# Reordering the four-tile borders of a two-block transformer kernel: which engine scales which operand block, and when

## The reference

```python
def adaln_in(s, g_pre, shift, scale):
    return rmsnorm(s, g_pre) * (1 + scale) + shift
def adaln_out(s, y, g_post, gate, weight):
    return s + weight * gate * rmsnorm(y, g_post)
def ffn_sublayer(s, mod, j, g_pre, g_post, wg, wu, wd):
    y = adaln_in(s, g_pre, mod[..., 3 * j, :, :], mod[..., 3 * j + 1, :, :])
    return adaln_out(s, swiglu(y, wg, wu, wd), g_post, mod[..., 3 * j + 2, :, :], FFN_RES)
for l in range(DEPTH):          # for x and, but for the last sublayers, for the context h
    x = ffn_sublayer(x, mod_x, 0, *f0)
    ...                         # a mixer: gMLP, differential attention, window attention
    x = ffn_sublayer(x, mod_x, 2, *f1)
```

## Time and profile before

| | |
|---|---|
| Median of 3 runs (lowest, highest) | 2495.48 us (2495.12, 2497.25) |
| The profiled execution: time, span | 2497.8 us, 2496.0 us |
| TensorE matmul busy | 2414.0 us (97%) |
| VectorE busy | 1143.2 us (46%) |
| ScalarE busy | 1021.4 us (41%) |
| GpSimd busy | 166.4 us (7%) |
| Mean share of the DMA queue of the weights (16 engines) | 41.6% |
| Mean granted clock of TensorE, of full speed | 0.989 |

### The profile page before, as it was taken

The page is one execution under the profiler, slowest core; times in us unless marked ns, Lnnn a source line. Parts: engine busy times, 40 slices in busy tenths (PEclk is TensorE's granted clock), DMA queues, the critical chain, the costliest instruction groups (busy, mean ns, idle before and its releaser), DMA issues. The chain is left out here.

```text
span 2496.0 us, 29214 instructions
## 1 busy us (share of the span) xinstructions
PE 2414.0 (97%) x11296; PEld 1898.3 (76%) x11296; DVE 1143.2 (46%) x1900; ACT 1021.4 (41%) x1766; POOL 166.4 (7%) x205
## 2 busy tenths in 40 slices
PE   8999999999999999999989999999999999988998
PEld 6876788766877778877677777887778887766777
DVE  5654465634552223363656222345322335456555
ACT  6544456534542222354545222234322234445444
POOL 1200003000010000013001000001000000310000
PEclk9999999999999999999989999999999999999999
DMA  6567654387535442232104444332532222322554
GB/s 213 189 231 277 234 186 152 121 309 279 187 129 185 172 140 93 85 97 98 51 18 143 178 169 169 102 101 85 175 123 99 93 85 93 119 68 77 184 187 143
DMA packets 118728, 364.34 MB, mean 146 GB/s; under 512 B 11072, under 2 KB 11712, under 8 KB 118592
## 3 DMA queue, kind: packets, MB, share of 16 engines
q1 hardware_dynamic: 116336, 355.62, 41.6%
q0 software_dynamic: 2256, 6.86, 1.0%
HBM read 361.35 MB, written 1.09 MB: 145 GB/s over the span
## 5 line engine op out<-in xcount | busy, mean ns | idle before, releaser
L1680 DVE TENSOR_TENSOR wlo<-raw,whi 128x1024 fp32r<-128x1024 f32 x524 | 644.0, 1234 | 731.6 <-ACT whi L1119 727.4
L1119 ACT CAST whi<-raw 128x1024 fp32r<-128x1024 f32 x524 | 548.2, 1050 | 621.2 <-PE ps L589 607.5
L589 PE MATMUL ps<-whi,xhi 128*128 128x512 f32 x1136 | 469.2, 413 | 26.6 <-ACT fbuf L1149 14.3
L589 PE MATMUL ps<-wlo,xhi 128*128 128x512 f32 x1136 | 449.4, 396 | 0.0
L589 PE MATMUL ps<-xhi,whi 128*128 128x512 f32 x960 | 378.8, 395 | 0.0
L589 PE MATMUL ps<-whi,ahi 128*128 128x512 f32 x952 | 374.6, 394 | 2.1 <-DVE wlo L1680 1.5
L589 PE MATMUL ps<-xhi,wlo 128*128 128x512 f32 x960 | 373.8, 389 | 0.0
L589 PE MATMUL ps<-xlo,whi 128*128 128x512 f32 x960 | 373.6, 389 | 0.0
L589 PE MATMUL ps<-wlo,ahi 128*128 128x512 f32 x952 | 372.0, 391 | 0.0
L589 PE MATMUL ps<-whi,xlo 128*128 128x512 f32 x1136 | 338.9, 394 | 0.0
L589 PEld LDWEIGHTS ps<-whi,xhi 128*128 128x128 f32 x1136 | 216.7, 191 | 101.4 <-issue 46.8
(11 more groups left out here) (163 smaller groups left out, 1658.2 us busy)
## 6 DMA issues: line engine op xcount, KB each, us to landing
raw<-in_w SPq DMA_DIRECT2D x524, 512.0 KB, 3.4
mraw<-in_w_mod SPq DMA_DIRECT2D x72, 1024.0 KB, 6.6
grow<-gains POOLq DMA_DIRECT2D x11, 512.0 KB, 6.8
x<-in_x SPq DMA_DIRECT2D x2, 512.0 KB, 5.4
x<-in_ctx SPq DMA_DIRECT2D x1, 1024.0 KB, 7.8
out<-x SPq DMA_DIRECT2D x2, 512.0 KB, 2.6
rmask<-in_rmask SPq DMA_DIRECT2D x1, 768.0 KB, 5.0
ws<-in_ws POOLq DMA_DIRECT2D x2, 256.0 KB, 7.0
```

The source lines that it names most:

```text
L589: return nc.tensor.matmul(o, lhsT, rhs, start=start, stop=stop, skip_group_check=True)
L1119: nc.scalar.copy(whi[:, slot, :], raw[:, slot, :]).then_inc(hi_done, 1)
L1680: nc.vector.tensor_tensor(wlo[:, slot, :], raw[:, slot, :], whi[:, slot, :].bitcast(F32), ALU.subtract).then_inc(w_split, 1)
```

## The change

In `operand_hi` and `operand_lo` ScalarE now scales blocks 2, 3, 4 and 5 and VectorE blocks 0, 1, 6 and 7, for every stage with four tiles in its wide part (4 to 8), the lead and the trail. The waits of `high` and `low` on `f_act` and `f_ready` are renumbered to that. On ScalarE the scalings of blocks 2 and 3 stand first, followed by the casts of blocks 0 to 3, scalings 4 and 5, the split of weight unit 2 and casts 4 and 5; only then come the square of the trail's tile 0 and the squares of its tile 1. On VectorE the addition of the trail's tile 0 moves from `turn`, ahead of the lead's operand, to a place behind low blocks 0 and 1 and the split of unit 1. The mean square of tile 0 and `out_tile` of tile 1 stand ahead of scalings 6 and 7, and `normed_tile` of tile 0 behind low blocks 4 and 5. Each four-tile wide stage is entered through these two functions; at the border 3 to 4 and for the trail's operand they run without the `trail` parts.

```diff
--- before.py
+++ after.py
@@ -1152,30 +1152,27 @@
                                              scale=acol[:, ctx_of(tiles), k:k + 1]).then_inc(f_act, 1)
 
                     def high(k):
-                        if k % 4 < 2:
-                            act.wait_ge(f_ready, s["f0"][st] + 2 * (k // 4) + k % 2 + 1)
+                        if 2 <= k < 6:
+                            act.wait_ge(f_act, s["f_act0"][st] + k - 1)
                         else:
-                            act.wait_ge(f_act, s["f_act0"][st] + 2 * (k // 4) + k % 2 + 1)
+                            act.wait_ge(f_ready, s["f0"][st] + (k + 1 if k < 2 else k - 3))
                         nc.scalar.copy(xhi[:, k, at0:at0 + w], fbuf[:, 256 * (k % 4):256 * (k % 4) + 256]).then_inc(xhi_ready, 1)
 
                     scaled(2)
-                    high(0)
-                    high(1)
+                    scaled(3)
+                    for k in range(4):
+                        high(k)
+                    scaled(4)
+                    scaled(5)
+                    if st == LEAD:
+                        split_hi(s["u_wide"] + 2)
+                    high(4)
+                    high(5)
                     if trail:
                         square_x(trail["tall"][TRAIL][0], X_AT[trail["i"], trail["tall"][TRAIL][0]])
-                    scaled(3)
-                    high(2)
-                    if st == LEAD:
-                        split_hi(s["u_wide"] + 2)
-                    high(3)
-                    if trail:
                         square_tile(trail, TRAIL, 1)
-                    for k in (4, 5):
-                        high(k)
                     if st == LEAD:
                         split_hi(s["u_wide"] + 3)
-                    scaled(6)
-                    scaled(7)
                     high(6)
                     high(7)
                     if trail:
@@ -1740,8 +1737,8 @@
 
                     def low(k):
                         dve.wait_ge(xhi_ready, n["xhi"] + k + 1)
-                        if k % 4 >= 2:
-                            dve.wait_ge(f_act, s["f_act0"][st] + 2 * (k // 4) + k % 2 + 1)
+                        if 2 <= k < 6:
+                            dve.wait_ge(f_act, s["f_act0"][st] + k - 1)
                         nc.vector.tensor_tensor(xlo[:, k, at0:at0 + w], fbuf[:, 256 * (k % 4):256 * (k % 4) + 256],
                                                 xhi[:, k, at0:at0 + w].bitcast(F32), ALU.subtract).then_inc(xs_ready, 1)
 
@@ -1750,21 +1747,22 @@
                     low(0)
                     low(1)
                     if trail:
-                        mean_square(trail["tall"][TRAIL][0])
                         split_lo(s["u_wide"] + 1)
-                    dve.wait_ge(xs_ready, s["xs0"][st] + 2)
-                    scaled(4)
-                    scaled(5)
+                        add_tile(trail, TRAIL, 0)
                     low(2)
+                    low(3)
                     if st == LEAD:
                         split_lo(s["u_wide"] + 2)
-                    low(3)
                     if trail:
-                        normed_tile(trail, TRAIL, 0)
+                        mean_square(trail["tall"][TRAIL][0])
                         out_tile(trail, TRAIL, 1)
+                    dve.wait_ge(xs_ready, s["xs0"][st] + 4)
+                    scaled(6)
+                    scaled(7)
                     low(4)
                     low(5)
                     if trail:
+                        normed_tile(trail, TRAIL, 0)
                         add_tile(trail, TRAIL, 1)
                     if st == LEAD:
                         split_lo(s["u_wide"] + 3)
@@ -1877,7 +1875,6 @@
                         normed_tile(s, LEAD, 1)
                         out_tile(s, TRAIL, 0)
                         split_lo(first)
-                        add_tile(s, TRAIL, 0)
                     operand_lo(nxt, st, s if st == LEAD else None)
                     return
                 if nxt["blk"] == 1:
```

## The result

| | Kernel before | Changed kernel |
|---|---|---|
| Median, 12 runs each (lowest, highest) | 2496.58 us (2495.07, 2498.15) | 2501.49 us (2493.95, 2508.55) |
| Ratio to before, 95% interval | | 1.0021 [1.0013, 1.0029] |
| Profiled execution: time, span | 2497.8, 2496.0 us | 2504.7, 2502.9 us |
| TensorE busy, mean granted clock | 2414.0 us, 0.989 | 2423.3 us, 0.985 |

The change made the kernel 4.9 us slower, and its median is 1.5 us above the predicted range. Of these 1.5 us, 1.1 come from the kernel before, whose median is 2496.58 us here and was 2495.48 in the three runs that the forecast started from. A second set on another occasion gave 1.0018 [1.0007, 1.0030]. The scatter grew too: 14.6 us from the lowest to the highest run instead of 3.1 (in larger sets, of 21 to 35 runs, the kernel before spreads over 6.7 to 8.3 us).

What follows compares the result with a forecast made beforehand. It took VectorE's in-order chain, ending in tile 1's normed rows, to bound each four-tile border. Chain -4.2, border 3 to 4 +1.0 and clock +3.7 gave +0.5 us: 2496.0 us, range 2491.5 to 2500.0.

Steps and rivals of the forecast that it cites:

- The lead's start: TensorE's pause before the lead's first matmul at each four-tile border: falls from 3.25 to 0.55 us, 2.7 us won there.
- VectorE's queue: VectorE's chain to tile 1's normed rows at each four-tile border: waits shrink, gaining 1.05 us, -4.2 us over four.
- TensorE between: TensorE from the lead's start to tile 1's transposes: waits 0.2 us for low block 5, then 3.4 us for tile 1.
- The clock: Behind the pause before tile 1's transposes: half clock at 2.7 of 4 borders, 1.39 us each, +3.7 us.
- The border 3 to 4: VectorE waits 1.4 us for unit 2's split, transposes come 1.3 us later; +1.0 us in the time.
- The trailing operand: Trail's operand, while TensorE is in unit 3: scaling 3 earlier, casts 0 and 1 about 0.4 us later; cost nothing.
- a rival of 0.18: Pause before tile 1's transposes: clock falls for double stretches; all four single 2497.9 us, all double 2503.4; chance 0.18.

Runs made afterwards that it cites:

- both repairs: Changed kernel with eleven unread matmuls before tile 1's transposes at the four borders, and the old order of scalings, casts and low parts at stage 4; 2491.53 us, ratio 0.9984.
- the old border 3 to 4: Changed kernel with the old order of scalings, casts and low parts at stage 4's operands alone; 2496.95 us, ratio 1.0009.
- the addition back: Changed kernel with the addition of the trail's tile 0 back in front of the lead's scalings on VectorE; 2502.64 us, ratio 1.0027.
- Unit 3 as the filler: Changed kernel with TensorE doing the lead's unit 3 ahead of the trail's sixteen transposes at the four borders; 2498.43 us, ratio 1.0011.
- the start pause filled: Kernel before with eleven unread 128x512 matmuls in its start pause of 3.3 us at the four borders; 2496.16 us, ratio 1.0001.
- the filler: Changed kernel with eleven unread 128x512 matmuls between the transposes of the trail's tiles 0 and 1 at the four borders; 2492.99 us, ratio 0.9993.

## Why the prediction was wrong

**The lead's start: right.** 0.50 to 0.54 us against 0.55.

**VectorE's queue: right.** Distance 13.45 us against 13.4 to 13.5, and 3.8 us in the time by the experiment with both repairs against 4.2.

**TensorE between: right.** A pause of 3.14 against 3.4 us (3.3 to 3.5 was named as the sign), 0.18 us before the low blocks against 0.2.

**The clock: the mechanism right, its size wrong; this is the step that failed.** The text took "the same share: 2.7 of 4 borders at 1.39, +3.7 us". Measured: 7.4 us, the difference between the changed kernel and the one with the pause filled (10.0 us in the profile). Both factors were too small. The profiles of the four kernels that keep the 3.1 us pause (the changed one twice, the old border 3 to 4, the addition back) hold sixteen such pauses; fourteen were followed by half clock, eight times for 3.4 us and six times for 6.8 us. At 1.62 and 2.8 us that is 14/4 x (8 x 1.62 + 6 x 2.8) / 14 = 7.4 us a run. That it meets the measured 7.4 so closely is partly luck: these four profiled executions took 3.3, 2.8 and 2.7 us more and 1.5 us less than the medians of their kernels, and the first three (the changed kernel twice, the old border 3 to 4) also lose 2.0 to 2.1 us against the profile before behind 2150 us, in the two further stretches of half clock near 2249 and 2293 us, which stand in no term of the sum. Unit 3 as the filler has them too, the other seven profiles don't; why they come is open. The prediction had 2.7 falls instead of 3.5, at 1.39 instead of 2.1 us. The 1.39 was the price of border 4 to 5 of the kernel before, a fall of 3.4 us; paid in full such a fall costs 1.60 to 1.64, close to half of 3.4. The double length was missing from the sum altogether. The rows at 709 and 1265 us had shown it, and the prediction named them, but as a rival of 0.18, with 0.04 above 2500.5 us.

What makes a stretch long was not tried by itself, and the prediction's reason, the short transposes behind the pause, is not enough. In the sixteen pauses the six long stretches all began before the pause ended, and the eight short ones after it, with the same transposes behind each. Border 3 to 4 repeats this behind its pauses of 3.5 and 5.3 us, again with the same sixteen transposes: in nine profiles the fall began before the end of the pause and lasted 6.8 us, in two (the old border 3 to 4, the start pause filled) it began 0.5 and 1.5 us after it and lasted 3.4. It is no general rule either: at 1265 us of the kernel before the fall began 1.7 us after the pause and lasted 6.8 us, and at border 4 to 5 of unit 3 as the filler it began 0.2 us before the end of the pause, with 128x512 matmuls behind it, and lasted 3.4.

**The border 3 to 4: right in the trace, a little low in the time.** +1.33 us on the way to the transposes against +1.3. In the time it is 1.5 to 1.7 us by the medians, against 1.0. From the last tall matmul to the wide matmuls at full clock, the seven profiles with the new order there take 0.5 to 1.5 us more than the profile before, 1.1 in the mean. Three others that keep the old order and the place of the transposes take from 0.9 us less to 0.1 more, so that new and old are 1.3 to 1.4 us apart in the mean. The half clock gave back a part in single executions, 0.8 us in the profile of the changed kernel, and nothing on average.

**The trailing operand: right.** With the clock up, 48 matmuls from tile 1's transposes on take what they took before.

With the measured terms the sum is -3.8 + 1.6 + 7.4 = +5.2 us, and measured were +4.9 and +5.2. This is no check of its own: the three terms are the steps from the kernel before over both repairs and the filler to the changed kernel, so they must add up to its difference. What checks them are the traces: 13.45 us at the borders, and the falls counted and priced.

## What to carry to other kernels

A pause of the bounding engine is worth what its removal moves at the next place where that engine waits. Before moving a pause, ask what is behind it: slack that a slower clock can use up, or nothing. Where a long pause has to stay, split it, or put real work into it, and check that this work's own inputs come ahead in the other queues.

## What the hardware showed that I had not expected

- Where the clock falls differs from run to run of one program, and a kernel with 3.1 us pauses ahead of bound work scatters by 15 us (12 runs), with 1.5 us pauses by 3.2 us (11 runs).
- A pause of 2.2 us brought the clock down at two of four borders, 1.5 us at none of four, 3.1 us at fourteen of sixteen; in the kernel before, 3.3 us did at two of four, and with unit 3 as the filler 1.8 us did at three of four.
- A stretch of half clock of 3.4 us costs 1.60 to 1.64 us, of 6.8 us that began 0.8 to 1.1 us before the end of the pause 2.65 to 2.87 us, where TensorE is the bound. Behind the start pause of the kernel before, where VectorE's chain is the bound, a stretch of 3.4 us cost 0.01 us at most.
- Eleven matmuls whose product nobody reads made a kernel 7.4 us faster.
